# Two-block transformer chain on one core: where the modulation rows are reduced, who squares, and how the output stage starts

## The chip, the cores and the metric

The kernel runs on one core of a Trainium2 chip. The time is device microseconds (us) of one execution, from the core's first to its last instruction and a little around it. Of each version several executions are timed; one more is profiled, and all rows below come from that one.

## The reference, cut to what matters

The input is one sequence of 512 positions and 1024 features, held feature-major. Two stacks of two layers follow each other; everything is float32.

```
for l in range(2):                                       # first stack ("block 1")
    mod = silu(c) @ ada_w[l] + ada_b[l]                  # 9 vectors of 1024
    h += 0.5*mod * swiglu(norm(h), ffn_w_in[l,0], ffn_w_out[l,0])     # d_ff 2816
    z = norm(h) @ mix_w_in[l]                            # q,k,v | gates | u,v | two merge gates
    y_a = attention(...);  y_b = u * (W_s layernorm(v) + b)
    merged = sigmoid(zga)*(y_a @ proj_a) + sigmoid(zgb)*(y_b @ proj_b)
    h += mod * (merged @ w_out)
    h += 0.5*mod * swiglu(norm(h), ffn_w_in[l,1], ffn_w_out[l,1])
h = norm(h)
for i in range(2):                                       # second stack
    mod = silu(c_2) @ w_ada[i] + b_ada[i]; the same with c_ctx_2      # 6 vectors each
    x += gate * norm(mixer(norm(x)))                     # i=0: pooling, i=1: attention
    x += gate * norm(square(relu(norm(x) @ w_mlp_in)) @ w_mlp_out)    # d_ff 4096
```

In the first layer of the second stack a context of 256 positions goes through the same pooling and the same MLP as the latents. `mod` is a matrix times one vector: 240 "rows", each a block of 128 output features by 1024 inputs.

## The kernel before, in words

**Products.** Each float32 product is made of three: high times high, high times low and low times high, where a high part is the value rounded to `fp32r` and a low part what is left. TensorE (PE) so runs three matmuls per 128-row block (lines L584 to L586, and L958 to L960 and L1007 to L1009 in the first pair of tiles of a network, L1218 to L1220 in the last tiles of one). The tiles `WH`, `WL` are the parts of a weight, `nH`, `nL` of a normed input, `hH`, `hL` of a hidden tile, `mH`, `mL` of the merged activations, `ybH`, `ybL` of the gated branch.

**Slots.** All large weights come as 308 slots in a fixed list, each 128 partitions by up to 2048 elements. A slot goes through three steps: SyncE (SP) issues its DMA into one of two `raw` buffers, ScalarE (ACT) makes `WH` (L476), VectorE (DVE) makes `WL` (L489), each in one of four buffers. The main loops of ACT, DVE and GpSimd (POOL) advance one slot at a time (`step_act`, `step_dve`, `step_pool`); in step k they split slot k+3, and that needs slot k-1 to be used up. SP in turn k issues slot k+5, and for that waits for both parts of slot k+3, which has the same `raw` buffer. In 18 of the slots of the context MLP POOL makes `WL` (L501).

**Rows.** The modulation rows are no work for TensorE. DVE multiplies a row tile `araw` with the broadcast condition `cB` and sums (L550). Rows 144 to 207 are needed for two conditions, and take two half operations into PSUM (L559), a small sum (L563) and L550. There are two `araw` buffers. `rows_after(k)` says how many rows are done by the end of step k: one more in each step, none in steps 196 to 231. In step k DVE first splits, then reduces the rows, then does the step's other work. SP issues in turn k, behind slot k+5, the rows up to one beyond those of step k, and each waits until DVE is done with the row two before it (`row(j)` in `sp_program`).

**A network of block 1** (`ffn_pe`, `ffn_act`, `ffn_dve`) has 33 slots. A round of six is: an a-step (two gate tiles, ACT: Silu, L1061), a b-step (two value tiles, DVE: product, L1112; ACT: high part, L1068; DVE: low part, L1118), again a and b, and two o-steps (four output tiles each, of the group of hidden tiles before; DVE adds them to `h`, L1185). All take their PSUM banks in turn from six. The middle networks are the second of layer 0 (slots 63 to 95) and the first of layer 1 (slots 96 to 128). Each ends with three slots in which all outputs are made in two halves of 256 positions (`network_end_pe`, "enter"), so that the next norm can begin.

**The MLPs of the second stack** use the same functions with `gated` false: ACT makes relu, DVE squares it (L1115), ACT makes the high part of the square, DVE the low part (L1118). The context's tiles are `scrc`, `hHc`, `hLc`, `mac`.

**The gated branch and the merge stage.** In `gmlp_dve` DVE evicts four tiles `sv` (L1821), multiplies (L1826) and makes low parts (L1828); PE makes `sv` in L1771 with only two free banks. The merge stage has sixteen slots; ACT makes a sigmoid in one tile `scr` (L1856), DVE multiplies (L1878, L1881), adds (L1884), ACT makes `mH` (L1861), DVE `mL` (L1886). `output_end_pe` then makes the output tiles one after another, each over all eight `mH`, `mL`.

Of the kernel before, what the change touches and what calls it, by code (L numbers as in the profile page):

```python
# [6 lines left out]
F32 = mybir.dt.float32  # L7
# [8 lines left out]
S = 512  # L16
# [78 lines left out]


SHARED = [0, 0]
CHANGE = 8 * 18 - 16


def ada_plan():
# [239 lines left out]
def build(nc, A, out):  # L341
# [3 lines left out]
    with ctx:  # L345
# [157 lines left out]

        def rows_after(k):

            idle = max(0, min(k, SHARED[1] - 1) - SHARED[0] + 1)
            late = min(2, max(0, k - CHANGE + 1))
            return min(8 * len(adas), 17 + k - idle - late)  # L510

        def row_tile(j):
            return M.rows[j] if j < NE else M.araw[j % NA]
# [537 lines left out]
        def ffn_act(act, g, p, nf, gated, hH, open_end=False):  # L1051
            N = p.N
            chunks = ffn_chunks(nf)
            order = [(ci, f) for ci, (f0, cn) in enumerate(chunks) for f in range(cn)]

            def first(ci, f):
                n = 4 * ci + f
                act.wait_ge(*mm.to(g, "a", ci, f))
                if n >= 2:
                    act.wait_ge(*v_pr.to(g, "b", *order[n - 2]))  # L1060
                act.q.activation(p.scr[n % 2][:, 0:N], bank(g, "a", ci, f)[:, 0:N],  # L1061
                                 ACT.Silu if gated else ACT.Relu).then_inc(*empties(a_fn, g, "a", ci, f))
# [35 lines left out]
        def ffn_dve(dve, g, p, nf, gated, hH, hL, sink, open_end=False):  # L1098
# [4 lines left out]
            def product(ci, f):  # L1103
# [10 lines left out]
                else:  # L1114
                    dve.q.tensor_tensor(p.scr[2 + u][:, 0:N], p.scr[u][:, 0:N], p.scr[u][:, 0:N],  # L1115
                                        ALU.mult).then_inc(*v_pr.up(g, "b", ci, f))
                dve.wait_ge(*a_hhi.to(g, ci, f))
                dve.q.tensor_tensor(hL[:, ci % 2, f, :], p.scr[2 + u][:, 0:N], hH[:, ci % 2, f, :].bitcast(F32),  # L1118
                                    ALU.subtract).then_inc(*v_hlo.up(g, ci, f))

            def second(ci):
# [107 lines left out]
        def output_end_pe(g):  # L1229
# [3 lines left out]

            def group(pe, x, o):
                k, c = k0 + o // 2, lat.half[x].cols
                b, free = take(g, "O", x, o)
                pe.wait_ge(*a_whi.to(k))
                pe.wait_ge(*wlo(k))
# [1 line left out]
                         lambda i: (a_hhi.to(g, "m", i), v_hlo.to(g, "m", i)), (g, "O", x, o), free)  # L1240
                if x and o % 2:
                    mm.again("slot", k)
            return group


# [11 lines left out]
        def enter_act(act, l, j):  # L1257
# [4 lines left out]
            rows_act(act, rows_after(k0) + 1)  # L1262
            both_halves_act(act, g, mod(1, l, 3 * j), lambda x, i: v_h.to(prev, "O", x, i),
                            output_ahead(k0) if j == 2 else network_ahead(k0))

        def enter_dve(dve, l, j):
# [528 lines left out]
        def gmlp_dve(dve, g, l):  # L1795
# [19 lines left out]
            step_dve(dve)  # L1815
            step_dve(dve)
            dve.wait_ge(*ld_bsb.to(l))
            for f in range(4):
                v = M.vf[:, f, :].rearrange("p (a b) -> p a b", a=4)
                dve.wait_ge(*mm.to(g, "sv", f))  # L1820
                dve.q.tensor_tensor(v, bank(g, "sv", f)[:, :].rearrange("p (a b) -> p a b", a=4),  # L1821
                                    M.bsb[:, f, :].unsqueeze(1).broadcast_to([128, 4, 128]), ALU.add
                                    ).then_inc(*empties(v_ev, g, "sv", f))
                dve.wait_ge(*v_ev.to(g, "sv", f))
                dve.wait_ge(*a_ev.to(g, "uv", f))
                dve.q.tensor_tensor(M.vf[:, f, :], M.vf[:, f, :], M.uu[:, f, :], ALU.mult).then_inc(*v_ev.up(g, "uv", f))  # L1826
                dve.wait_ge(*a_yhi.to(g, "yb", f))
                dve.q.tensor_tensor(M.ybL[:, f, :], M.vf[:, f, :], M.ybH[:, f, :].bitcast(F32), ALU.subtract  # L1828
                                    ).then_inc(*v_ylo.up(g, "yb", f))

        def gmlp_pool(pool, g, l):
            pool.wait_ge(*mm.to(g, "v", 7, 0))
# [9 lines left out]
                                 ALU.mult).then_inc(*p_wT.up(g))  # L1842

        def merged_act(act, g):
            sg = lat.scr[0]
            before = None
            for m in range(4):
                for which in range(2):
                    if m or which:
                        step_act(act)  # L1850
                        step_act(act)
                    for f in (2 * m, 2 * m + 1):
                        act.wait_ge(*mm.to(g, "z", which, f))
# [4 lines left out]
                        before = (g, "sum", f) if which else (g, "p", 0, f)  # L1858
                        if which:
                            act.wait_ge(*v_mg.to(g, "sum", f))  # L1860
                            act.q.activation(M.mH[:, f, :], lat.scr[1 + f % 2][:, :], ACT.Copy  # L1861
                                             ).then_inc(*a_hhi.up(g, "m", f))

        def merged_dve(dve, g):
            sg = lat.scr[0]
            for m in range(4):
                for which in range(2):
                    if m or which:
                        step_dve(dve)
                        step_dve(dve)  # L1870
                    for f in (2 * m, 2 * m + 1):
                        y = lat.scr[1 + f % 2]
# [759 lines left out]
        def sp_program(sp):  # L2632
# [33 lines left out]
            loaded = 16  # L2666
            for k in range(len(slots)):
                if k == CHANGE:
# [136 lines left out]
```

## Time and profile before

| | |
|---|---|
| median of 3 executions | 3921.39 us (3918.61 to 3925.29) |
| profiled execution, its own time | 3915.16 us |
| its span | 3913.4 us |
| mean granted TensorE clock | 0.962 |
| PE busy | 3668.9 us (94%) |
| DVE busy | 2231.8 us (57%) |
| ACT busy | 1311.4 us (34%) |
| POOL busy | 341.8 us (9%) |
| moved by DMA | 451.93 MB, 115 GB/s over the span |

The matmuls overlap in this view, so "PE busy" is the time in which at least one is in the array; what PE loses is seen where a matmul row names an idle time before it. The two clock levels are 2.4 GHz (1.0) and 1.2 GHz (0.5).

### The profile page before, as it was taken

The page shows a single profiled execution, that of the slowest core. Times are in us where ns is not written, and L with a number is a line of the kernel's source. Part 1 is how long each engine was busy: PE and PEld are TensorE (multiplying, and loading weights), DVE is VectorE, ACT ScalarE, POOL GpSimd, SP SyncE. Part 2 cuts the span into 40 slices and gives each one's busy share as a digit, 9 for nine tenths or more (in the row PEclk, how much of TensorE's full clock was granted, in tenths as well). Part 3 has the DMA queues.
Part 4 walks back from the last instruction along what each step waited for, and adds up shares of the span by engine and source line. Part 5 has one row for each costly group of instructions (what it writes and reads, how often), then busy time and mean ns, then how long its engine had stood idle before and what let it go on. Part 6 is the DMA issues. An engine that isn't in the chain of part 4 may idle for free.

```text
span 3913.4 us, 45537 instructions
## 1 busy us (share of the span) xinstructions
PE 3668.9 (94%) x18026; PEld 2962.2 (76%) x18026; DVE 2231.8 (57%) x3607; ACT 1311.4 (34%) x1906; POOL 341.8 (9%) x380
## 2 busy tenths in 40 slices
PE   6999899999999999999999999887799969999997
PEld 5888856788889888855788878777588846577886
DVE  5554644656446545554666767776755555634444
ACT  3222443233223222444224323344322234533221
POOL 0000122000001000112001010134100010200000
PEclk9999999999999999989999999998899968999998
DMA  5433301334432433310343434333233311012221
GB/s 225 167 145 145 120 33 59 127 137 164 146 145 102 183 139 144 126 69 25 124 162 124 149 143 161 124 119 140 87 145 145 135 49 54 1 44 85 89 97 42
DMA packets 84228, 451.93 MB, mean 115 GB/s; under 512 B 10193, under 2 KB 10641, under 8 KB 47153
## 3 DMA queue, kind: packets, MB, share of 16 engines
q1 hardware_dynamic: 81936, 439.35, 30.5%
q0 software_dynamic: 2080, 9.67, 0.7%
q8 instruction: 144, 2.36, 0.2%
q14 instruction: 68, 0.55, 0.0%
HBM read 446.88 MB, written 2.10 MB: 115 GB/s over the span
## 4 chain that ended last, share of the span: by engine, by line
PE 80%; DVE 9%; issue 4%; ACT 4%; DMA 1%; POOL 1%; SPq 0%; DVEq 0%; POOLq 0%; ACTq 0%
PE ps L584 21%; PE ps L586 21%; PE ps L585 21%; PE ps L1453 3%; PE ps L1489 2%; ACT WH L476 1%; DVE WL L489 1%; DVE scrc L1115 1%; PE ps L2418 1%; PE ps L1471 1%; DMA araw<-in_ast 1%; DVE scr L661 1%; PE ps L2392 1%; PE ps L958 1%; PE ps L604 1%
## 5 line engine op out<-in xcount | busy, mean ns | idle before, releaser
L584 PE MATMUL ps<-nH,WH 128*128 128x512 f32 x2416 | 956.9, 396 | 9.2 <-DVE nL L716 7.1
L489 DVE TENSOR_TENSOR WL<-raw,WH 128x2048 fp32r<-128x2048 f32 (+2 forms) x290 | 639.2, 2208 | 555.8 <-ACT WH L476 554.7
L586 PE MATMUL ps<-nH,WL 128*128 128x512 f32 x2416 | 953.1, 395 | 0.0
L585 PE MATMUL ps<-nL,WH 128*128 128x512 f32 x2416 | 951.0, 394 | 0.0
L476 ACT ACTIVATE WH<-raw 128x2048 fp32r<-128x2048 f32 (+2 forms) x308 | 560.0, 1823 | 583.8 <-PE ps L586 554.4
L584 PEld LDWEIGHTS ps<-nH,WH 128*128 128x128 f32 x2416 | 457.7, 189 | 118.7 <-issue 10.4
L585 PEld LDWEIGHTS ps<-nL,WH 128*128 128x128 f32 x2416 | 457.6, 189 | 103.5 <-issue 2.2
L586 PEld LDWEIGHTS ps<-nH,WL 128*128 128x128 f32 x2416 | 457.3, 189 | 99.4
L584 PE MATMUL ps<-hH,WH 128*128 128x512 f32 x1072 | 422.2, 394 | 2.2 <-DVE h L1185 2.2
L586 PE MATMUL ps<-hH,WL 128*128 128x512 f32 x1072 | 421.8, 393 | 0.0
L585 PE MATMUL ps<-hL,WH 128*128 128x512 f32 x1072 | 421.5, 393 | 0.0
L550 DVE SCALAR_TENSOR_TENSOR araw<-araw,cB 128x1024 f32<-128x1024 f32 x225 | 276.5, 1229 | 73.3 <-DMA araw<-in_ast 73.2
L1068 ACT ACTIVATE hH<-scr 128x512 fp32r<-128x512 f32 x152 | 96.1, 632 | 456.7 <-DVE scr L1112 382.9
L584 PEld LDWEIGHTS ps<-hH,WH 128*128 128x128 f32 x1072 | 201.4, 188 | 48.5 <-DVE h L1185 2.7
L585 PEld LDWEIGHTS ps<-hL,WH 128*128 128x128 f32 x1072 | 201.4, 188 | 46.2
L586 PEld LDWEIGHTS ps<-hH,WL 128*128 128x128 f32 x1072 | 201.4, 188 | 46.2
L1061 ACT ACTIVATE scr<-ps 128x512 f32<-128x512 f32 x152 | 89.5, 595 | 387.5 <-PE ps L586 379.2
L931 POOL TENSOR_SCALAR scr<-scr,der,mods 128x256 f32<-128x256 f32 x80 | 61.8, 773 | 1532.9 <-DVE scr L844 1532.0
L1118 DVE TENSOR_TENSOR hL<-scr,hH 128x512 fp32r<-128x512 f32 x152 | 105.3, 692 | 106.1 <-ACT hH L1068 106.1
L1185 DVE SCALAR_TENSOR_TENSOR h<-ps,der,h 128x512 f32<-128x512 f32 x144 | 102.6, 747 | 66.9 <-PE ps L586 65.4
L2108 DVE TENSOR_TENSOR ma<-ma,ps 128x512 f32<-128x512 f32 x112 | 74.7, 684 | 111.6 <-PE ps L586 111.2
L1664 DVE TENSOR_REDUCE st<-ps 128x1 f32<-128x128 f32 (+3 forms) x128 | 62.0, 486 | 111.1 <-PE ps L1455 111.0
(357 smaller groups left out, 5432.6 us busy)
## 6 DMA issues: line engine op xcount, KB each, us to landing
raw<-in_wst SPq DMA_DIRECT2D x282, 1024.0 KB, 4.8
araw<-in_ast SPq DMA_DIRECT2D x225, 512.0 KB, 5.7
raw<-in_wst SPq DMA_DIRECT2D x18, 512.0 KB, 3.6
row<-in_ast SPq DMA_DIRECT2D x15, 512.0 KB, 15.0
cw<-in_cw POOLq DMA_DIRECT2D x4, 1024.0 KB, 6.0
h<-in_xT SPq DMA_DIRECT2D x1, 2048.0 KB, 8.3
raw<-in_wst SPq DMA_DIRECT2D x8, 256.0 KB, 2.6
out<-h SPq DMA_DIRECT2D x8, 256.0 KB, 2.0
```

What stands on the lines that cost most here:

```text
L476: act.q.activation(M.WH[k % NW][:, 0:n], M.raw[k % NR][:, 0:n], ACT.Copy).then_inc(*a_whi.up(k))
L489: dve.q.tensor_tensor(M.WL[k % NW][:, 0:n], M.raw[k % NR][:, 0:n], M.WH[k % NW][:, 0:n].bitcast(F32), ALU.subtract).then_inc(*v_wlo.up(k))
L550: dve.q.scalar_tensor_tensor(out=w[:, :], in0=w[:, :], scalar=1.0, in1=M.cB[q][:, :], op0=ALU.mult, op1=ALU.mult, accum_out=total).then_in ...
L584: pe.q.matmul(to, hi[:, i, cc], xh, start=i == 0, stop=False)
L585: pe.q.matmul(to, hi[:, i, cc], xl, start=False, stop=False)
L586: t = pe.q.matmul(to, lo[:, i, cc], xh, start=False, stop=i == nk - 1)
L1061: act.q.activation(p.scr[n % 2][:, 0:N], bank(g, "a", ci, f)[:, 0:N], ACT.Silu if gated else ACT.Relu).then_inc(*empties(a_fn, g, "a", ci, f))
L1068: act.q.activation(hH[:, ci % 2, f, :], p.scr[2 + f % 2][:, 0:N], ACT.Copy).then_inc(*a_hhi.up(g, ci, f))
L1118: dve.q.tensor_tensor(hL[:, ci % 2, f, :], p.scr[2 + u][:, 0:N], hH[:, ci % 2, f, :].bitcast(F32), ALU.subtract).then_inc(*v_hlo.up(g, ci, f))
L1185: dve.q.scalar_tensor_tensor(out=M.h[:, o, :], in0=bank(g, "o", ci, o)[:, :], scalar=gate[:, o:o + 1], in1=M.h[:, o, :], op0=ALU.mult, op1 ...
L1453: pe.q.matmul(b[:, 0:nk], M.q[half, hh // 2, 128 * qt:128 * qt + 128], K[half, 0:nk], start=True, stop=False, skip_group_check=True)
L1489: t = pe.q.matmul(to[half, 128 * x:512], M.Vt[br - 1][:, x, 64 * grp:64 * grp + 64], M.PT[br - 1][:, x, 128 * x:512], start=br == 1 and x ...
```

## The change

There are three parts, and two that go with them.

1. `rows_after(k)` reads a table made by `row_steps`. By it two rows are reduced in each step of the middle networks, and in every third step of layer 0's first network. None is reduced in the three last slots of a network (but for the fourth network, layer 1's second), in the first six slots of `mix_w_in`, in `proj_a`, `proj_b`, `w_out`, and in the first slots of the fourth network. The whole stays the same 240 rows. The extra row at the entry of a stage goes.
2. In the MLPs of the second stack ACT makes the high part as the square of relu itself, and no longer waits for DVE's product. In all networks DVE does two products and then two low parts.
3. The first four output tiles behind the merge stage are made together: all four over `mH`, `mL` 0 to 5, then all four over 6 and 7. It takes its four banks at once.
4. The merge stage uses two sigmoid tiles in turn, and in the gated branch the low part of a tile comes after the next tile's product.

```diff
-CHANGE = 8 * 18 - 16
+def row_steps(slots, total):
+    done, out, waited = 16, [], 0
+    for k, (a, idx, r0, nk, c0, n) in enumerate(slots):
+        more = 2 if a[:3] == "ffn" and (idx in ((0, 1), (1, 0)) or k % 3 == 0 and idx == (0, 0)) else 1
+        if a == "ffn_w_out" and r0 >= 16 * 128 and idx != (1, 1):
+            more = 0
+        if a == "ffn_w_in" and (c0 == NF * 128 or idx == (1, 1) and c0 % (NF * 128) < 512):
+            more = 0
+        if a == "mix_w_in" and c0 <= 1280 or a in ("proj_a", "proj_b", "w_out"):
+            more = 0
+        if SHARED[0] <= k < SHARED[1]:
+            more = 0
...
         def rows_after(k):
-            idle = max(0, min(k, SHARED[1] - 1) - SHARED[0] + 1)
-            late = min(2, max(0, k - CHANGE + 1))
-            return min(8 * len(adas), 17 + k - idle - late)
+            return row_plan[k]
...
             def high(ci, f):
-                act.wait_ge(*v_pr.to(g, "b", ci, f))
+                act.wait_ge(*(v_pr.to(g, "b", ci, f) if gated else a_fn.to(g, "a", ci, f)))
...
-                act.q.activation(hH[:, ci % 2, f, :], p.scr[2 + f % 2][:, 0:N], ACT.Copy).then_inc(*a_hhi.up(g, ci, f))
+                act.q.activation(hH[:, ci % 2, f, :], p.scr[(2 if gated else 0) + f % 2][:, 0:N],
+                                 ACT.Copy if gated else ACT.Square).then_inc(*a_hhi.up(g, ci, f))
...
                     product(ci, f)
                     product(ci, f + 1)
+                    low(ci, f)
+                    low(ci, f + 1)
...
+            def four(pe):
+                c, to = lat.half[0].cols, []
+                for o in range(4):
+                    b, free = take(g, "O", 0, o)
+                    pe.wait_ge(*free)
+                    to.append(b[:, 0:S // 2])
+                for part in (range(6), range(6, 8)):
+                    for o in range(4):
...
+                        for i in part:
+                            pe.wait_ge(*a_hhi.to(g, "m", i))
+                            pe.wait_ge(*v_hlo.to(g, "m", i))
...
-            rows_dve(dve, rows_after(k0) + 1)
+            rows_dve(dve, rows_after(k0))
...
         def merged_act(act, g):
-            sg = lat.scr[0]
-            before = None
+            before = [(), ()]
...
+                        sg = lat.scr[3 * (f % 2)]
                         act.wait_ge(*mm.to(g, "z", which, f))
-                        if before is not None:
-                            act.wait_ge(*v_mg.to(*before))
+                        if before[f % 2]:
+                            act.wait_ge(*v_mg.to(*before[f % 2]))
```

The order of the instructions shows part 1 in the middle networks. First SP, in the second network of layer 0, before the change; `raw` is a slot, `araw` a row, the number behind each name its buffer.

```order
L2647 DMA araw1_16<-in_ast 128x1024
L2639 DMA raw0_5<-in_wst 128x2048
L2647 DMA araw0_15<-in_ast 128x1024
L2639 DMA raw1_6<-in_wst 128x2048
L2647 DMA araw1_16<-in_ast 128x1024
```

The same place after the change:

```order
L2696 DMA raw1_6<-in_wst 128x2048
L2704 DMA araw0_15<-in_ast 128x1024
L2704 DMA araw1_16<-in_ast 128x1024
L2696 DMA raw0_5<-in_wst 128x2048
L2704 DMA araw0_15<-in_ast 128x1024
L2704 DMA araw1_16<-in_ast 128x1024
```

Two rows now stand behind each slot. DVE in the same network before the change, one a-step and one b-step:

```order
L489 TENSOR_TENSOR WL_13<-raw_5,WH_9 128x2048
L550 SCALAR_TENSOR_TENSOR araw_16,mods<-araw_16,cB_17 128x1024
L489 TENSOR_TENSOR WL_14<-raw_6,WH_10 128x2048
L550 SCALAR_TENSOR_TENSOR araw_15,mods<-araw_15,cB_17 128x1024
L1112 TENSOR_TENSOR scr_27<-scr_25,ps 128x512
L1118 TENSOR_TENSOR hL<-scr_27,hH 128x512
L1112 TENSOR_TENSOR scr_28<-scr_26,ps 128x512
L1118 TENSOR_TENSOR hL<-scr_28,hH 128x512
```

And after it:

```order
L512 TENSOR_TENSOR WL_13<-raw_5,WH_9 128x2048
L572 SCALAR_TENSOR_TENSOR araw_16,mods<-araw_16,cB_17 128x1024
L572 SCALAR_TENSOR_TENSOR araw_15,mods<-araw_15,cB_17 128x1024
L512 TENSOR_TENSOR WL_14<-raw_6,WH_10 128x2048
L572 SCALAR_TENSOR_TENSOR araw_16,mods<-araw_16,cB_17 128x1024
L572 SCALAR_TENSOR_TENSOR araw_15,mods<-araw_15,cB_17 128x1024
L1135 TENSOR_TENSOR scr_27<-scr_25,ps 128x512
L1135 TENSOR_TENSOR scr_28<-scr_26,ps 128x512
L1144 TENSOR_TENSOR hL<-scr_27,hH 128x512
L1144 TENSOR_TENSOR hL<-scr_28,hH 128x512
```

Each step has a second row, in the other `araw` buffer, ahead of the step's own work, and the low parts stand behind both products. ACT in the context's MLP, before the change, where `scrc_99` and `_100` hold relu and `scrc_101` and `_102` the squares:

```order
L476 ACTIVATE WH_7<-raw_5 128x2048
L1061 ACTIVATE scrc_99<-ps 128x256
L1068 ACTIVATE hHc<-scrc_101 128x256
L1061 ACTIVATE scrc_100<-ps 128x256
L1068 ACTIVATE hHc<-scrc_102 128x256
```

And after it:

```order
L499 ACTIVATE WH_7<-raw_5 128x2048
L1083 ACTIVATE scrc_99<-ps 128x256
L1090 ACTIVATE hHc<-scrc_99 128x256
L1083 ACTIVATE scrc_100<-ps 128x256
L1090 ACTIVATE hHc<-scrc_100 128x256
```

The order is the same; the high part now reads relu's own tile.

## Rows read from the trace of the kernel before

**Rows 1.** Windows: stretch, length, busy us per engine (count): PE, PEld, DVE, ACT, POOL; clock, DMA share, GB/s.
```profile
905.00:1205.00 300.00, 300.00 (x1318) 246.35 (x1317) 150.66 (x167) 78.27 (x71) 0.00 (x0) 1.00 0.42 156
...
2500.00:2755.00 255.00, 203.03 (x1470) 195.74 (x1470) 187.16 (x245) 106.01 (x145) 96.20 (x37) 0.89 0.37 130
...
839.00:843.00 4.00, 4.00 (x25) 4.00 (x25) 3.14 (x2) 2.24 (x3) 0.00 (x0) 0.65 0.00 0
```

**Rows 2.** Waits over the span: who for whom, us, times, longest.
```profile
DVE araw L550 <- DMA araw<-in_ast: 73.2, 24, 6.3
```

**Rows 3.** Timeline, DVE, entry behind layer 1's first network: start, us, engine, line, operation [idle before].
```profile
1586.72 1.22 DVE L550 SCALAR_TENSOR_TENSOR araw<-araw,cB 128x1024 f32<-128x1024 f32 x1
...
1593.03 1.23 DVE L550 SCALAR_TENSOR_TENSOR araw<-araw,cB 128x1024 f32<-128x1024 f32 x1 [5.08 <-DMA araw<-in_ast]
```

**Rows 4.** Timeline, SP, the same place.
```profile
1586.88 0.33 SPq L2639 DMA_DIRECT2D raw<-in_wst  x1
1587.25 0.43 SPq L2647 DMA_DIRECT2D araw<-in_ast  x1
```

**Rows 5.** DMA issues of 940 to 1180 (KB each, us to landing), and all row tiles.
```profile
raw<-in_wst SPq DMA_DIRECT2D x23, 1024.0 KB, 4.7
araw<-in_ast SPq DMA_DIRECT2D x23, 512.0 KB, 5.7
DMA to landing us min/median/max: 3.4/5.7/15.1
```

**Rows 6.** Timeline, DVE, one b-step.
```profile
1007.79 2.29 DVE L489 TENSOR_TENSOR WL<-raw,WH 128x2048 fp32r<-128x2048 f32 x1 [8.01 <-ACT WH L476]
...
1011.26 0.69 DVE L1112 TENSOR_TENSOR scr<-scr,ps 128x512 f32<-128x512 f32 x1
...
1016.34 0.69 DVE L1112 TENSOR_TENSOR scr<-scr,ps 128x512 f32<-128x512 f32 x1 [3.01 <-PE ps L586]
...
1019.60 2.29 DVE L489 TENSOR_TENSOR WL<-raw,WH 128x2048 fp32r<-128x2048 f32 x1 [1.18 <-ACT WH L476]
```

**Rows 7.** Groups by line, DVE, 940 to 1180: count, busy us, mean ns, idle before.
```profile
L1185 DVE SCALAR_TENSOR_TENSOR h<-ps,der,h 128x512 f32<-128x512 f32 x27 | 19.5, 748 | 15.9 <-PE ps L586 15.6
```

**Rows 8.** Timeline, DVE, a row for two conditions, and what follows it.
```profile
1639.12 0.69 DVE L559 SCALAR_TENSOR_TENSOR ps<-araw,cB 128x512 f32<-128x512 f32 x1
...
1641.89 1.16 DVE L1595 COPY R<-cm 64x496 f32<-64x496 f32 x2
```

**Rows 9.** Timeline, DVE, the first steps of layer 0's second network.
```profile
904.17 1.22 DVE L550 SCALAR_TENSOR_TENSOR araw<-araw,cB 128x1024 f32<-128x1024 f32 x1
```

**Rows 10.** Timeline, PE, the same place: the first row behind the wide pair.
```profile
906.17 0.40 PE L584 MATMUL ps<-nH,WH 128*128 128x512 f32 x1
```

**Rows 11.** Timeline, DVE, the first compression of layer 0.
```profile
445.13 2.33 DVE L1595 COPY R<-cm 64x496 f32<-64x496 f32 x4
```

**Rows 12.** Timeline, PE, the same place.
```profile
448.83 1.51 PE L1378 MATMUL ps<-R,cw 128*128 128x62 f32 x6 [9.29 <-DVE R L1599]
```

**Rows 13.** Timeline, PE, the gated branch of layer 0.
```profile
711.32 1.58 PE L1771 MATMUL ps<-wT,vn 128*64 128x128 f32 x16 [2.43 <-DVE vf L1821]
...
716.84 0.47 PE L584 MATMUL ps<-nH,WH 128*128 128x512 f32 x1 [1.23 <-DVE vf L1821]
```

**Rows 14.** Timeline, PE, the first output tile behind layer 0's merge stage.
```profile
836.11 0.36 PE L584 MATMUL ps<-mH,WH 128*128 128x256 f32 x1 [0.86 <-DVE mL L1886]
...
838.82 0.36 PE L584 MATMUL ps<-mH,WH 128*128 128x256 f32 x1 [2.12 <-DVE mL L1886]
```

**Rows 15.** Timeline, PE, the context's first sum.
```profile
2150.60 0.99 PE L619 MATMUL ps<-ones,scrc 128*128 128x1 f32 x4 [8.85 <-DVE scrc L661]
```

**Rows 16.** Timeline, DVE, the context's MLP.
```profile
2602.36 4.75 DVE L1115 TENSOR_TENSOR scrc<-scrc 128x256 f32<-128x256 f32 x1 [1.38 <-ACT scrc L1061]
...
2638.40 0.42 DVE L1115 TENSOR_TENSOR scrc<-scrc 128x256 f32<-128x256 f32 x1
```

**Rows 17.** Timeline, POOL, the same place.
```profile
2602.23 4.60 POOL L501 TENSOR_TENSOR WL<-raw,WH 128x2048 fp32r<-128x2048 f32 x1 [6.47 <-PE ps L586]
```

More of the change, by code:

```diff
@@ L97 @@
 SHARED = [0, 0]
-CHANGE = 8 * 18 - 16
+def row_steps(slots, total):
[10 more added lines that the diff above has]
+            more = 0
+        if done == 8 * 18 and waited < 2:
+            more, waited = 0, waited + 1
+        elif done < 8 * 18:
+            more = min(more, 8 * 18 - done)
+        done = min(total, done + more)
+        out.append(done)
+    return out
 def ada_plan():
@@ L502, in split_pool @@
                                      ALU.subtract).then_inc(*p_wlo.up(k))
+        row_plan = row_steps(slots, 8 * len(adas))
         def rows_after(k):
-            idle = max(0, min(k, SHARED[1] - 1) - SHARED[0] + 1)
-            late = min(2, max(0, k - CHANGE + 1))
-            return min(8 * len(adas), 17 + k - idle - late)
+            return row_plan[k]
         def row_tile(j):
@@ L1116, in product, with low @@
                                         ALU.mult).then_inc(*v_pr.up(g, "b", ci, f))
+            def low(ci, f):
                 dve.wait_ge(*a_hhi.to(g, ci, f))
-                dve.q.tensor_tensor(hL[:, ci % 2, f, :], p.scr[2 + u][:, 0:N], hH[:, ci % 2, f, :].bitcast(F32),
+                dve.wait_ge(*v_pr.to(g, "b", ci, f))
+                dve.q.tensor_tensor(hL[:, ci % 2, f, :], p.scr[2 + f % 2][:, 0:N], hH[:, ci % 2, f, :].bitcast(F32),
                                     ALU.subtract).then_inc(*v_hlo.up(g, ci, f))
@@ L1235, in group @@
                 k, c = k0 + o // 2, lat.half[x].cols
+                if x == 0 and o < 4:
+                    if o == 0:
+                        four(pe)
+                    return
                 b, free = take(g, "O", x, o)
@@ L1242, in group @@
                     mm.again("slot", k)
+            def four(pe):
[6 more added lines that the diff above has]
+                    for o in range(4):
+                        k = k0 + o // 2
+                        pe.wait_ge(*a_whi.to(k))
+                        pe.wait_ge(*wlo(k))
+                        hi, lo, cc = view(M.WH, k), view(M.WL, k), slice(o % 2 * 128, o % 2 * 128 + 128)
+                        for i in part:
+                            pe.wait_ge(*a_hhi.to(g, "m", i))
+                            pe.wait_ge(*v_hlo.to(g, "m", i))
+                            pe.q.matmul(to[o], hi[:, i, cc], M.mH[:, i, c], start=i == 0, stop=False,
+                                        skip_group_check=True)
+                            pe.q.matmul(to[o], hi[:, i, cc], M.mL[:, i, c], start=False, stop=False, skip_group_check=True)
+                            t = pe.q.matmul(to[o], lo[:, i, cc], M.mH[:, i, c], start=False, stop=i == 7,
+                                            skip_group_check=True)
+                        if i == 7:
+                            t.then_inc(*mm.up(g, "O", 0, o))
             return group
@@ L1261, in enter_act @@
             split_act(act, k0 + NW)
-            rows_act(act, rows_after(k0) + 1)
+            rows_act(act, rows_after(k0))
             both_halves_act(act, g, mod(1, l, 3 * j), lambda x, i: v_h.to(prev, "O", x, i),
@@ L1817, in gmlp_dve @@
             dve.wait_ge(*ld_bsb.to(l))
[L1818 to L1829, printed above, removed]
+            for f in range(5):
+                if f < 4:
+                    v = M.vf[:, f, :].rearrange("p (a b) -> p a b", a=4)
+                    dve.wait_ge(*mm.to(g, "sv", f))
+                    dve.q.tensor_tensor(v, bank(g, "sv", f)[:, :].rearrange("p (a b) -> p a b", a=4),
+                                        M.bsb[:, f, :].unsqueeze(1).broadcast_to([128, 4, 128]), ALU.add
+                                        ).then_inc(*empties(v_ev, g, "sv", f))
+                    dve.wait_ge(*v_ev.to(g, "sv", f))
+                    dve.wait_ge(*a_ev.to(g, "uv", f))
+                    dve.q.tensor_tensor(M.vf[:, f, :], M.vf[:, f, :], M.uu[:, f, :], ALU.mult).then_inc(*v_ev.up(g, "uv", f))
+                if f:
+                    dve.wait_ge(*a_yhi.to(g, "yb", f - 1))
+                    dve.q.tensor_tensor(M.ybL[:, f - 1, :], M.vf[:, f - 1, :], M.ybH[:, f - 1, :].bitcast(F32), ALU.subtract
+                                        ).then_inc(*v_ylo.up(g, "yb", f - 1))
         def gmlp_pool(pool, g, l):
@@ L1852, in merged_act @@
                     for f in (2 * m, 2 * m + 1):
+                        sg = lat.scr[3 * (f % 2)]
                         act.wait_ge(*mm.to(g, "z", which, f))
-                        if before is not None:
-                            act.wait_ge(*v_mg.to(*before))
+                        if before[f % 2]:
+                            act.wait_ge(*v_mg.to(*before[f % 2]))
                         act.q.activation(sg[:, :], bank(g, "z", which, f)[:, :], ACT.Sigmoid
                                          ).then_inc(*empties(a_fn, g, "z", which, f))
-                        before = (g, "sum", f) if which else (g, "p", 0, f)
+                        before[f % 2] = (g, "sum", f) if which else (g, "p", 0, f)
                         if which:
@@ L1864, in merged_dve @@
         def merged_dve(dve, g):
-            sg = lat.scr[0]
             for m in range(4):
@@ L1871, in merged_dve @@
                     for f in (2 * m, 2 * m + 1):
-                        y = lat.scr[1 + f % 2]
+                        y, sg = lat.scr[1 + f % 2], lat.scr[3 * (f % 2)]
                         dve.wait_ge(*a_fn.to(g, "z", which, f))
@@ L2665, in sp_program @@
                 raw(k)
-            loaded = 16
+            loaded, changed = 16, False
             for k in range(len(slots)):
-                if k == CHANGE:
+                if loaded == 8 * 18 + 1 and k and row_plan[k - 1] == 8 * 18 and not changed:
+                    changed = True
                     sp.wait_ge(*v_row.to(8 * 18 - 1))
```

## The prediction

> **What bounds the kernel now.** I read the clock and busy shares first, then windows of the stages, then the waits and the timelines behind them. The reader is to see that the kernel has two kinds of stages. In the middle networks PE has no idle time: 300 of 300 us busy, 1318 matmuls, 0.228 us each, DVE busy half the time [rows 1]. A slot of 48 matmuls is 10.98 us there, a round of six slots 65.9 us. So a step that DVE finishes sooner gains nothing, and DVE has 5 us a step to spare, if nothing makes it wait. Elsewhere PE waits: 52 of 255 us in the context's MLP [rows 1], and singly at the compression, in the gated branch and behind the merge stage [rows 12 to 14]. The question is whether DVE can take two rows a step in its spare time, and what their absence gives the other places.
>
> **Two rows a step.** DVE's time for the extra row, 1.26 us (1011.26 less 1007.79 less the 2.21 of the split [rows 6]), would fit. The wait for its data doesn't. With two `araw` buffers the step's second row can be issued only when the row two before is done, and SP has it behind the slot of the same turn, whose issue waits for `WL` of this very step. The trace has this case at stage entries, where two rows stand in one step: SP issues the slot 0.16 us after the first row has begun and the row 0.37 later [rows 4], it lands after 5.7 us, the median [rows 5], and the second row starts 6.31 us after the first, 5.08 of them idle [rows 3]. Between the bounds of 4.0 (the fastest landing, 3.4, with the 0.5 of issue before it) and 16 (the slowest, 15.1) I take 6.31, since it is this very sequence and agrees with the median; 24 such waits average 3.05 us [rows 2], but that counts single rows too.
>
> DVE's chain from split to split is then, in an a-step, 2.21 + 6.31 + 1.27 = 9.79 us; in a b-step 0.65 (first product) and 3.26 more, from the second product over the high part and ACT's next `WH` to the next split (1016.34 to 1019.60 [rows 6]): 13.7; in an o-step four sums of 0.7 (748 ns with its overlap [rows 7]): 12.6. A round is 2 x (9.79 + 13.7 + 12.6) = 72.2 against PE's 65.9. DVE falls back 6.3 us a round and becomes the bound. With rows for two conditions (144 to 207) the second takes 2.77 instead of 1.27 (1639.12 to 1641.89 [rows 8]); the first's longer time lies beside the landing. That is 1.5 more a step, 81.2 a round, 15.3 too long.
>
> Layer 0's second network: 28 double steps, slots 65 to 92 (10 a, 10 b, 8 o), 335.7 us. They begin late: the last split before ends at 904.17 [rows 9], two rows take until 911.8, then come the wide pair's products, so that the next split starts near 915.7, 10 after PE has left the wide pair at 906.17 [rows 10]. The first two splits come together (2.2 more), and a row then stands behind two slots, for which I estimate 1.6 more, little over the 1.3 by which 1 MB takes longer than the fastest row [rows 5]: 3.8. The last low part is made before a further split, 1.2 less. PE needs 28 x 10.98 = 307.4, and can do 1.4 us of the last slots first. Loss: 335.7 + 10 + 3.8 - 1.2 - 307.4 - 1.4 = 39.5.
>
> Layer 1's first network: eight double steps reach slot 104 some 16 us late, of which 3.9 is hidden: a sum into `h` ends that long before PE takes its bank again (the third output tile takes that of the first, 24 matmuls or 5.5 us later, less 1.6 of sums). 12 are paid. Slots 106 to 108 have one row or none and reset it. Slots 109 to 125 are 17 double steps with heavy rows (5 a, 6 b, 6 o): 49 + 82 + 76 + 17 x 1.5 = 232.3 against 186.7: 45. Together 57. PE's clock falls behind a long wait: right behind the waits in front of the first output tile it is 0.65 over 4 us [rows 1, 14], a loss of 1.4. I add 3 for the two network ends and take off 2 for waits that are there today. Sum of part 1's cost: 39.5 + 57 + 3 - 2 = 97, called 96 for the rounding of the small terms.
>
> The third-step extras in the first network cost nothing: a single late step per six is 1 to 2 us behind in a slot's 11, and the next ones catch up.
>
> **What the missing rows give.** At layer 0's compression DVE copies at 445.13 [rows 11], behind a burst of rows; without them it could at 439.2. PE starts at 448.83 [rows 12] and would at 442.7: 6.1, in layer 1 about 1. In the gated branch row and row wait go from between the tiles, and product stands ahead of low part: of waits like 2.43 and 1.23 [rows 13] nearly all goes, and the next product starts at 712.2 instead of 716.84: 4.7 a layer, 9.5. At the context's first sum PE waits 8.85 [rows 15]; without the row before the last squares 4.5 go. Other places with heavy rows: 2. Sum 23; the bounds are 10 (only the compression and half the branch) and 32 (every one of these waits gone).
>
> **Four output tiles together.** The waits of 0.86 and 2.12 [rows 14], 0.3 in others, and 1.7 of clock go, since PE has 72 matmuls of parts 0 to 5 before it needs 6. But it takes four banks at once; the fourth is that of a sigmoid which ACT makes in sequence near the end: a new wait of 1.6. Behind it stands all of PE, and nothing else is late. 3.6 in layer 0, 6.8 in layer 1, 10.4. Bounds: 4 (waiting 4.8 per layer) and 14.
>
> **High part by ACT.** ACT goes from relu's tile straight to the square, and needs no table for it (the norms' squares stand between relus today without one), so it costs nothing there; ACT is busy 106 of 255 us [rows 1]. What goes is the way over DVE, some 0.5 us per tile, more where DVE's product takes 4.75 instead of 0.42 us [rows 16] beside POOL's `WL` [rows 17]. PE waits for `hLc` all the same, which needs that product and the low part. Of 52 us I give it 10; bounds 0 and 25.
>
> That DVE product is what the Trainium skill ("GPSIMD Engine Reference", section "Specifications") would have: GpSimd shares its way to SBUF with VectorE, against instructions with two SBUF inputs. The trace agrees, 4.75 beside POOL against 0.42. By it only the high part gets out of the way, product and low part don't, which speaks against a gain much over 10.
>
> **Sum.** 3915.2 (the profiled execution's own time) + 96 - 23 - 10.4 - 10 = 3968. The median of the runs is 6 above the profiled one, which is not more than their spread; I take 3970.
>
> **Rivals.**
> A, the rows are hidden after all, faster. The chain fits into PE's round when the second row starts less than 5.28 us after the first (72.2 - 6 x 1.03 = 66). With the fastest landing, 3.4, it is 4.0, and a round takes 58 (68 heavy): loss 0 to 5, time 3921 - 43 + 3 = 3881. For it: the landing needed is only 1.03 shorter than the median, and the extra rows have shorter ones at times [rows 5]. Against it: in rows 3 a slot of 1 MB stands ahead of the row, as it would in every step, and that slot alone takes 4.7 [rows 5].
> B, only the heavy stretch pays: the first network's 38 are hidden by slots and banks prepared ahead. 3970 - 38 = 3932, still slower. For it: DVE idles 8.01 before a split [rows 6], so much slack there is at the start; against it: 39 is more than slack of that size.
> C, three transfers in a turn slow each other: landing 7.2 instead of 5.7, 0.5 MB more ahead of the row at the 1.3 us between the fastest row and a slot [rows 5], and a little. 1.5 x 50 steps = 75: 4045. For it: the slowest landing of 15.1; against it: the third is behind the second in one queue, and the queue is busy 42% of the time [rows 1].
> D, the gains don't come (the banks of the four tiles and POOL take them back), 20 instead of 43: 3993.
>
> The Trainium skill ("DMA: Bandwidth & Descriptors", section "Bandwidth") has 6.15 us for 1 MB, where the trace shows 4.7 [rows 5]. By it the row would come 1.4 later in 50 steps, an estimate of 70 us more, about 4040; the case is C's and has its chance. The measurement decides, so that the page is no part of the sum.
>
> **Numbers.** Forecast 0.58, A 0.15, B 0.11, C 0.08, D 0.08. Less than 0.2%, 8 us, can't be told from no change. Faster: A and little else, 0.16; within: the lower edge of B and the upper of A, 0.07; slower: 0.77. The forecast's own range is 3945 to 3995 (landing 0.3 us shorter or longer is 15). For 8 in 10 it reaches over B down to 3912 and up to 4012; A and C's upper part are left out.
>
> **What would show it.** DVE idle about 5 us for the row before the second of each pair, in some 55 steps; DVE's splits 36 us apart per three steps instead of 33; PE waiting at the third output tile of a round (a bank emptied by late sums) and for the last low parts at the network's ends, and a lower clock behind it; windows of the two networks some 39 and 57 us longer. On the other side: the compression's wait 9.3 down to about 3; no waits at the branch; a wait of 1.6 before the four tiles; the context's high part no more behind the product. The forecast is wrong if the wait before the second row is under 4 us, or if PE's matmuls in the networks stay at 0.229 us throughout.

## The result, and the profile after

| | before | after |
|---|---|---|
| median | 3920.0 us (3918.2 to 3925.29, 4 runs) | 3956.27 us (3953.55 to 3962.54, 4 runs) |
| ratio | 1 | 1.0093 (1.0075 to 1.011) |
| span of the profiled execution | 3913.4 us | 3952.6 us |
| clock | 0.962 | 0.959 |
| DVE waits for a row's DMA (L550/L572) | 73.2 us, 24 times [rows 2] | 257.9 us, 51 times |

The change makes the kernel 36 us slower. The forecast was 3970, inside 3912 to 4012. The two waits of DVE for rows after the change are these (who for whom, us in total, times, longest):

```profile
DVE araw L572 <- DMA araw<-in_ast: 257.9, 51, 7.2
DVE ps L581 <- DMA araw<-in_ast: 63.2, 18, 4.1
```

The first is what [rows 2] were before, three and a half times as much; the second is the same for rows with two conditions. The windows of the two middle networks and of the context's MLP (columns as in [rows 1]; the stretches are where these parts lie in the changed kernel):

```profile
890.00:1230.00 340.00, 316.08 (x1340) 257.26 (x1340) 180.30 (x222) 77.55 (x71) 0.00 (x0) 0.96 0.47 178
1284.00:1670.00 386.00, 340.86 (x1501) 280.04 (x1500) 243.17 (x411) 92.16 (x88) 5.63 (x8) 0.94 0.42 158
2556.00:2792.00 236.00, 202.22 (x1495) 195.47 (x1493) 183.32 (x239) 106.78 (x143) 95.53 (x37) 0.91 0.39 139
```

[rows 1] have layer 0's second network and the MLP; layer 1's first network was this, before:

```profile
1275.00:1585.00 310.00, 309.40 (x1366) 254.28 (x1365) 155.34 (x170) 81.22 (x73) 0.00 (x0) 1.00 0.41 152
```

PE, with 0 and 0.6 us of idle time before, is idle for 24 of 340 us in the first and 45 of 386 in the second; in the MLP it has 34 us of idle time in 236 where it had 52 in 255. Both profiles have the same number of matmuls, 18026, so that the same matmul can be looked up in each and its start subtracted. That gives where the 39 us between the profiles come from:

| stretch (time in the kernel before) | forecast | measured |
|---|---|---|
| layer 0, compression (430 to 450) | -6.1 | -6.6 |
| gated branch, layer 0 and 1 | -4.7, -4.7 | -4.7, -5.0 |
| merge stage's end and output tiles, layer 0 and 1 | -3.6, -6.8 | -1.8, -3.7 |
| layer 0's second network (906 to 1270) | +39.5 | +40.3 |
| layer 1's first network (1270 to 1640) | +57 | +58.8 |
| context's first sum (2135 to 2160) | -4.5 | -10.9 |
| context's MLP (2475 to 2780) | -10 | -18.0 |
| all else | -3 (and +1 in the networks, not split) | -9 |

The steps can be read one by one. DVE in a b-step and the a-step behind it, in layer 0's second network of the changed kernel (start, us, engine, line, operation, idle before):

```profile
1082.62 2.29 DVE L512 TENSOR_TENSOR WL<-raw,WH 128x2048 fp32r<-128x2048 f32 x1
1084.83 1.22 DVE L572 SCALAR_TENSOR_TENSOR araw<-araw,cB 128x1024 f32<-128x1024 f32 x1
...
1091.11 1.22 DVE L572 SCALAR_TENSOR_TENSOR araw<-araw,cB 128x1024 f32<-128x1024 f32 x1 [5.06 <-DMA araw<-in_ast]
1092.38 1.28 DVE L1135 TENSOR_TENSOR scr<-scr,ps 128x512 f32<-128x512 f32 x2
1093.77 1.29 DVE L1144 TENSOR_TENSOR hL<-scr,hH 128x512 fp32r<-128x512 f32 x2
1096.24 2.29 DVE L512 TENSOR_TENSOR WL<-raw,WH 128x2048 fp32r<-128x2048 f32 x1 [1.18 <-ACT WH L499]
1098.45 1.22 DVE L572 SCALAR_TENSOR_TENSOR araw<-araw,cB 128x1024 f32<-128x1024 f32 x1
...
1106.18 2.29 DVE L512 TENSOR_TENSOR WL<-raw,WH 128x2048 fp32r<-128x2048 f32 x1
```

SP in the same place:

```profile
1084.98 0.33 SPq L2696 DMA_DIRECT2D raw<-in_wst  x1
1085.36 1.05 SPq L2704 DMA_DIRECT2D araw<-in_ast  x2
```

The second row starts 6.28 us after the first (1084.83 to 1091.11), 5.06 of them idle, as at the stage entry of before (6.31 [rows 3]). SP issues the slot at 1084.98, 0.15 after the first row has begun (0.16 in [rows 4]), and two rows behind it, where [rows 4] had one. The first of the two is the row that DVE waits for. From split to split the b-step takes 13.62 us and the a-step 9.94; the forecast had 13.7 and 9.79. PE in the same kernel, at the third output tile of some rounds of either network, and at the last slots of both:

```profile
986.34 0.79 PE L606 MATMUL ps<-hH,WH 128*128 128x512 f32 x1 [5.97 <-DVE h L1213]
...
1058.46 0.50 PE L606 MATMUL ps<-hH,WH 128*128 128x512 f32 x1 [3.87 <-DVE h L1213]
...
1239.76 0.36 PE L1246 MATMUL ps<-hH,WH 128*128 128x256 f32 x1 [4.34 <-DVE hL L1144]
...
1544.98 0.80 PE L606 MATMUL ps<-hH,WH 128*128 128x512 f32 x1 [7.81 <-DVE h L1213]
...
1625.66 0.80 PE L606 MATMUL ps<-hH,WH 128*128 128x512 f32 x1 [7.71 <-DVE h L1213]
...
1666.21 0.55 PE L1246 MATMUL ps<-hH,WH 128*128 128x256 f32 x1 [9.81 <-DVE hL L1144]
```

The tile waits for DVE's sum, which empties its bank (5.97 and 7.81), the last slots for the last low part (4.34 and 9.81). A round of six slots took PE 72.1 us (986.34 to 1058.46), one with heavy rows 80.7 (1544.98 to 1625.66); DVE's chain was forecast at 72.2 and 81.2.

PE's waits explain only part of the loss. There are six of them in layer 0's second network, 28.3 us in all, and eight in layer 1's first, 45.1 us. The other 26 of the 99 us are matmuls at the lower of the two clock levels, right behind the waits. The window behind the wait of 5.97:

```profile
986.00:990.00 4.00, 3.66 (x9) 2.89 (x10) 4.00 (x5) 0.00 (x0) 0.00 (x0) 0.50 0.02 4
```

By 994 the clock is back at 1.00. On the side of the gains, PE at the compression, in the gated branch and in front of the four output tiles:

```profile
443.28 3.00 PE L1434 MATMUL ps<-R,cw 128*128 128x62 f32 x19 [3.33 <-DVE R L1655]
...
703.71 0.47 PE L606 MATMUL ps<-nH,WH 128*128 128x512 f32 x1 [0.44 <-DVE vf L1878]
...
821.66 0.36 PE L1292 MATMUL ps<-mH,WH 128*128 128x256 f32 x1 [1.64 <-DVE mL L1943]
```

The 9.29 of [rows 12] are 3.33, the 1.23 of [rows 13] 0.44, and the two waits of [rows 14] have become one of 1.64, about what the forecast put for the new wait of the four tiles. The 8.85 of [rows 15] are gone altogether.

### The profile page after: what moved, and what is told of

It is laid out like the page before. It is cut to its first block, busy times and chain, and to the rows that moved or that the text cites. A ratio compares the mean times of both kernels' runs of the same rounds, so it can differ in the third digit from the quotient of the medians.

```text
span 3952.6 us, 45843 instructions
## 1 busy us (share of the span) xinstructions
PE 3681.7 (93%) x18026; PEld 2972.0 (75%) x18026; DVE 2219.2 (56%) x3607; ACT 1311.8 (33%) x1906; POOL 342.0 (9%) x380
## 4 chain that ended last, share of the span: by engine, by line
PE 66%; DVE 12%; DMA 9%; issue 7%; ACT 5%; POOL 1%; SPq 0%; DVEq 0%; POOLq 0%; ACTq 0%
PE ps L606 16%; PE ps L608 16%; PE ps L607 16%; DMA araw<-in_ast 8%; DVE WL L512 4%; PE ps L1509 3%; ACT WH L499 2%; PE ps L1545 2%; PE ps L2475 1%; PE ps L1527 1%; PE ps L1246 1%; PE ps L1248 1%; PE ps L1247 1%; DVE ps L581 1%; DVE h L1213 1%
## 5 line engine op out<-in xcount | busy, mean ns | idle before, releaser
L606 PE MATMUL ps<-hH,WH 128*128 128x512 f32 x1072 | 433.1, 404 | 61.5 <-DVE h L1213 46.4
L572 DVE SCALAR_TENSOR_TENSOR araw<-araw,cB 128x1024 f32<-128x1024 f32 x225 | 276.7, 1230 | 258.0 <-DMA araw<-in_ast 257.9
L1138 DVE TENSOR_TENSOR scr<-scr 128x512 f32<-128x512 f32 x64 | 48.2, 756 | 158.4 <-ACT scr L1083 156.1
L581 DVE SCALAR_TENSOR_TENSOR ps<-araw,cB 128x512 f32<-128x512 f32 x128 | 88.6, 733 | 63.2 <-DMA araw<-in_ast 63.2
```

The costliest lines, as they stand in the source:

```text
L572: dve.q.scalar_tensor_tensor(out=w[:, :], in0=w[:, :], scalar=1.0, in1=M.cB[q][:, :], op0=ALU.mult, op1=ALU.mult, accum_out=total).then_in ...
L581: dve.q.scalar_tensor_tensor(out=banks[6 + x][:, :], in0=w[:, cut], scalar=1.0, in1=M.cB[q][:, cut], op0=ALU.mult, op1=ALU.mult, accum_out ...
L606: pe.q.matmul(to, hi[:, i, cc], xh, start=i == 0, stop=False)
```

## The experiments

All medians below are compared with the kernel before on the same chip (3918 to 3920 us); the ratio is to it. "Matmul by matmul" means the stretches of the table above, in the profiled executions.

### The parts without the row plan, and the row plan alone

The first kernel is the changed one with the rows as before:

```diff
-            return row_plan[k]
+            idle = max(0, min(k, SHARED[1] - 1) - SHARED[0] + 1)
+            late = min(2, max(0, k - CHANGE + 1))
+            return min(8 * len(adas), 17 + k - idle - late)
...
-            rows_dve(dve, rows_after(k0))
+            rows_dve(dve, rows_after(k0) + 1)
```

> The changed kernel with the rows of the kernel before (one per step, with the extra one at stage entries), so only squares, four tiles, two sigmoid tiles and the order of low parts are left of the change. Theory (the middle networks lose by the wait for each step's second row): both networks as before, no loss there (PE 0.229 us per matmul throughout); what is left is the context's MLP, up to 18 us, and the output stages, about 5: 3920 - 23 = 3897, range 3890 to 3908. Rival (product, product, low, low is what delays the networks): still 30 us or more lost in the two networks, about 3925 or more.

Measured: 3889.53 us (3888.2 to 3891.92), ratio 0.9931 (0.9915 to 0.9948). The rival is out: the networks take what they took before to within 1 us. The time is half a us under the range. Matmul by matmul, 18 to 19 us of the gain lie in the context's MLP (by where the stretch is begun), 2.5 at the context's first sum, 2.3 in the gated branches, 0.5 in layer 0's output stage and nothing in layer 1's.

The second is the kernel before with `row_steps` and without the rest:

```diff
-            return min(8 * len(adas), 17 + k - idle - late)
+            return row_plan[k]
```

> The kernel before with the new row plan alone. Theory: loses 99 us in the two middle networks (40 and 59) and gains some 30 at the compression, gated branch and the context's first sum: 3920 + 69 = 3989, range 3975 to 4000. Rival (the low parts' new order or the four tiles have a part in the loss): under 3975.

Measured: 4007.19 us (3996.29 to 4016.93), ratio 1.0229 (1.0204 to 1.0254). That is outside both expectations, on the far side. Matmul by matmul the networks lose 56.7 and 75.8 us, not 40 and 59. What is left between this and the changed kernel in the networks is the order of products and low parts; it has a part in the time, but the one opposite to the rival's. The experiment with that order alone is below. The gains of the rows alone are 6.6 at the compression, 10.9 at the context's first sum, 0.4 and 4.7 at the output stages, 2.6 and 2.8 in the gated branches: there rows and order are worth 4.7 and 5.0 together, and the order alone 0.9 and 1.5 (the first experiment).

### The rows ahead of the slot

Here SP issues the rows that step k reduces itself before slot k+5. The row waits only for the last row of step k-1, the slot for this step's split.

```diff
+                while loaded < rows_after(k):
+                    row(loaded)
+                    loaded += 1
                 if k + NR + NW - 1 < len(slots):
                     raw(k + NR + NW - 1)
```

> The changed kernel, where SP issues the rows that step k itself reduces ahead of slot k+5 instead of behind it; same rows, same buffers, same work on every other engine. Theory (the second row of a pair comes late because its issue stands behind a slot's, which waits for this step's own split): the second row is issued when the last row of the step before is done, about 3.5 us before it is wanted in an a-step and more in others; DVE's round falls from 72 to about 45 us, under PE's 65.9, and the networks' 99 us come back: 3956 - 97 = 3859, range 3850 to 3875. Rival 1 (DVE's own extra work and the queue's load are the cost): no more than 20 back, above 3935. Rival 2 (a row ahead of the slot delays the slots): the networks gain less, 3880 to 3920, with ACT waiting for raw.

Measured: 3855.0 us (3849.73 to 3855.97), ratio 0.9838 (0.9824 to 0.9853), as the theory had it, and far from both rivals. DVE in layer 0's second network of this kernel, one b-step:

```profile
1062.85 2.29 DVE L512 TENSOR_TENSOR WL<-raw,WH 128x2048 fp32r<-128x2048 f32 x1 [6.74 <-ACT WH L499]
1065.06 1.22 DVE L572 SCALAR_TENSOR_TENSOR araw<-araw,cB 128x1024 f32<-128x1024 f32 x1
1066.32 1.23 DVE L572 SCALAR_TENSOR_TENSOR araw<-araw,cB 128x1024 f32<-128x1024 f32 x1
1067.58 0.69 DVE L1135 TENSOR_TENSOR scr<-scr,ps 128x512 f32<-128x512 f32 x1
1071.40 0.69 DVE L1135 TENSOR_TENSOR scr<-scr,ps 128x512 f32<-128x512 f32 x1 [3.13 <-PE ps L608]
```

SP in the same place:

```profile
1065.21 0.33 SPq L2696 DMA_DIRECT2D raw<-in_wst  x1
1066.31 1.59 SPq L2704 DMA_DIRECT2D araw<-in_ast  x2
```

The second row now starts 1.26 us after the first, with no idle time, and DVE waits for PE again (3.13). The rows go out when a row is done (1066.31), and both are in the queue before the next slot. The waits for rows fall to this:

```profile
DVE araw L572 <- DMA araw<-in_ast: 21.2, 9, 4.2
```

Same rows, same buffers, same work: from 906 to 1640 of the kernel before, the networks now take 1.4 us less than there, 100 us less than in the changed kernel (40.3 + 58.8 + 1.4). So the whole loss came from one order of issues on SP's queue, and the lower clock behind PE's waits went with the waits.

### The order of low parts, alone

The changed kernel, with product, low, product, low as before:

```diff
                     product(ci, f)
-                    product(ci, f + 1)
                     low(ci, f)
+                    product(ci, f + 1)
                     low(ci, f + 1)
```

> The changed kernel (3956.3) with product, low, product, low as before, nothing else. Theory (a b-step of the middle networks now is 1.4 to 3 us shorter on DVE's chain, which bounds there): the networks lose 33 us more, as the rows alone showed: 3956 + 33 = 3989, range 3980 to 3995. Rival (what the rows alone lost more came from elsewhere): within 8 of 3956.

Measured: 3984.86 us (3970.59 to 3986.59), ratio 1.016 (1.014 to 1.018). The two networks lose 31.3 us more matmul by matmul, theory 33. A b-step of DVE (1083.80 to 1098.84) takes 15.04 us instead of 13.62, with 0.70 of idle time for ACT's high part before each low part. So where DVE is the bound, making both products first is worth 31 us; where PE is, as in the kernel before, it is worth nothing (the networks of the first experiment).

### Squares by ACT

The changed kernel with the high part of a square again as a copy of DVE's product:

```diff
-                act.wait_ge(*(v_pr.to(g, "b", ci, f) if gated else a_fn.to(g, "a", ci, f)))
+                act.wait_ge(*v_pr.to(g, "b", ci, f))
```

> The changed kernel with ACT's high part of the squares again a copy of DVE's product, all else kept. Theory A (the context's MLP gained 18 us because the high part no longer waits for DVE's product beside POOL's splits): 3956 + 15 = 3971, range 3966 to 3978, the loss all in that MLP. Theory B (it gained by the other order of products and low parts): within 5 of 3956.

Measured: 3973.47 us (3971.38 to 3975.66), ratio 1.0144 (1.0128 to 1.0159), as theory A had it. 16.5 us are lost in the context's MLP, under 0.1 us in the 600 us before it. The two profiles are 21.0 us apart; 2.8 of it lie behind the context's MLP, where the latents' squares are too, and no experiment says whether these have a part in it. ACT's high parts there, of this kernel (count, busy us, mean ns, idle before and who ended it):

```profile
L1090 ACT ACTIVATE hHc<-scrc 128x256 fp32r<-128x256 f32 x30 | 12.5, 417 | 63.6 <-DVE scrc L1137 63.6
```

And of the changed one:

```profile
L1090 ACT ACTIVATE hHc<-scrc 128x256 fp32r<-128x256 f32 x29 | 12.1, 418 | 0.9
L1138 DVE TENSOR_TENSOR scrc<-scrc 128x256 f32<-128x256 f32 x30 | 43.2, 1478 | 13.5 <-ACT scrc L1083 13.5
```

63.6 us of idle time in front of ACT's high parts are 0.9. DVE's product is as slow as before, 1478 ns in the mean where the short ones take 0.42 us [rows 16], and 13.5 us of waits for relu stay, but the product no longer holds up ACT, which has the next `WH` and relu behind it. PE's waits show what that gives: for ACT's relu they fall from 7.0 us with the copy to 0.5, and for the sums of the norm beside it (L683) from 22.9 to 13.5. Those for DVE's sums into `mac` rise from 12.7 to 15.4. That was the missed part: I priced the way of one tile through DVE, not ACT's queue behind the waiting high part.

### The four output tiles

On the kernel with rows ahead of the slot (3855.0), first without the four tiles:

```diff
-                if x == 0 and o < 4:
-                    if o == 0:
-                        four(pe)
-                    return
```

> The kernel with rows ahead of the slot (3855.0), without the four output tiles made together: each tile again over all eight parts, one after another. Theory (the rows that no longer stand in w_out shortened the last chain by themselves, and the four tiles exchange one wait for another): within 4 us of 3855. Rival (as the prediction had it, the four tiles give 10): 3865.

Measured: 3857.13 us (3840.12 to 3864.22), ratio 0.9837 (0.9805 to 0.9869). The two medians come from two chips and the runs of this kernel spread over 24 us, so they say little; matmul by matmul in the two output stages the four tiles are worth 1.5 to 2.5 us, not 10. PE waits once in each layer here, 1.95 us. In layer 0:

```profile
825.33 0.36 PE L606 MATMUL ps<-mH,WH 128*128 128x256 f32 x1 [1.95 <-DVE mL L1939]
```

Before, it waited 0.86 and 2.12 there [rows 14]. The first of these waits is gone with the row plan alone too, so it went with the rows, and I had given it to the four tiles. The two sigmoid tiles were not taken out by themselves; no run shows their share. Then with the bank of each tile taken when its first matmul comes:

```diff
-                    pe.wait_ge(*free)
-                    to.append(b[:, 0:S // 2])
+                    to.append((b[:, 0:S // 2], free))
                 for part in (range(6), range(6, 8)):
                     for o in range(4):
+                        if 0 in part:
+                            pe.wait_ge(*to[o][1])
```

> The kernel with rows ahead of the slot (3855.0), where the four tiles take each its bank when its first matmul comes instead of all four at the start. Theory (the 1.64 us in front of the four is the wait for the fourth bank, whose sigmoid comes last): that wait goes in both layers, 3855 - 3.3 = 3851.7, and up to 3 more where the clock no longer dips. Rival (the wait is for mL, as the row names its releaser): 3855, the wait stays.

Measured: 3847.74 us (3834.6 to 3848.95), ratio 0.9811 (0.9792 to 0.9829). The wait of 1.64 is gone in both layers, no wait over 0.4 us is left there, and these stretches are 1.9 and 0.8 us shorter matmul by matmul. The median is 1 us under the lowest that was expected (3848.7). The row had named `mL` as its releaser; it was the bank. The kernel with both sigmoids ahead of both `mH`:

```diff
-                        if which:
-                            act.wait_ge(*v_mg.to(g, "sum", f))
+                    for f in (2 * m, 2 * m + 1) if which else ():
+                        act.wait_ge(*v_mg.to(g, "sum", f))
```

> The one before with ACT making both sigmoids of a pair ahead of both mH. Theory: the sigmoid that frees the last bank no longer stands behind mH; nothing waits for it any more with banks in turn, so within 2 us of it. Rival (the last mH and mL come late): 1 us of wait ahead of parts 6 and 7 in each layer goes or comes.

Measured: 3850.96 us (3842.91 to 3855.38), ratio 0.9824 (0.9807 to 0.9841). The median is 3.2 us above that of the one before, less than the spread of either, and the two output stages agree within 0.1 us matmul by matmul: no difference that can be told. Last, the two best once more, on one chip:

> The kernel with rows ahead of the slot once more, beside the next one on one chip, to compare the two: 3855, range 3849 to 3859.

Measured: 3857.57 us (3851.24 to 3861.12), ratio 0.9844 (0.9828 to 0.9861).

> The same with banks in turn once more. Theory (the wait of 1.64 and the lower clock behind it in both layers): 4 to 7 us under the one beside it. Rival (the 7 us between their first medians was the spread of the clock in the attention stages): within 3.

Measured: 3846.95 us (3836.94 to 3850.39), ratio 0.9812 (0.9792 to 0.9832). This is 10.6 us below its neighbour. Banks in turn has the lowest median, 1.9% below the kernel before and 2.8% below the changed one. But the 10.6 us are more than the 4 to 7 expected, and the profiled executions of this pair do not show them: they are 0.9 us apart (spans of 3849.4 and 3848.6), with 0.8 and 0.9 us gained in the two output stages. What the waits and the two stretches show for the banks is 2 to 3 us. A candidate for the rest is the clock in the attention stages (last section), and whether the shorter wait has any part in that wasn't settled.

## Why the prediction was right, and where it was off

**The bound and the wait.** Right, and shown: the second row 6.28 us after the first (forecast 6.31), chains of 13.62 and 9.94 (13.7 and 9.79), networks +40.3 and +58.8 (39.5 and 57). The row of one stage entry carried 100 us of the sum, because it was the same sequence of issues. Taking the slot out from before the row takes the whole loss away: the second row then starts 1.26 us after the first, and the networks lose nothing. So A named the right condition, which this change did not meet; its limit of 5.28 us was not tested. Two things the forecast had not named. PE waits also for banks that DVE's product (L1135) empties, 4.12 us once in layer 0's network and 2.87, 5.75 and 2.31 in layer 1's. And the lower clock stands behind all but one of PE's fourteen waits in the networks, 26 of the 99 us, where the forecast had it at their ends only, within its 3. Both shift where the delay is paid and not its sum: the forecast took the loss from DVE's chain, and PE's rounds came out as long as that chain.

**B and C.** Layer 0's second network lost its 40, so B is out. The rows landed 6.1 us after issue in the stretch with double rows, in the median, against 5.7 before [rows 5]:

```profile
raw<-in_wst SPq DMA_DIRECT2D x17, 1024.0 KB, 4.8
araw<-in_ast SPq DMA_DIRECT2D x34, 512.0 KB, 6.1
```

That includes each pair's other row, issued 0.7 later, whose landing nobody waits for. The waited-for row landed after 5.7 to 5.8 (1085.36 to 1091.1), the slot in 4.8. C is out. The 6.15 us that the Trainium skill gives for 1 MB ("DMA: Bandwidth & Descriptors", section "Bandwidth") were measured with transfers issued by GpSimd. This kernel has four such transfers of 1 MB, over the whole span:

```profile
cw<-in_cw POOLq DMA_DIRECT2D x4, 1024.0 KB, 5.9
```

These land after 5.9 us, near the page's figure, but the slots are issued by SyncE and land after 4.8. So the estimate of 70 us more, worked out from that figure, was for the wrong issuer, and did not come.

**The gains** were 60, not 43. The step that failed is "Of 52 us I give it 10" for the context's MLP: it was 18.0, of which the squares by ACT were 16.5. The rule of the Trainium skill ("GPSIMD Engine Reference", section "Specifications"), that GpSimd and VectorE share their way to SBUF, agrees with the product's 1478 ns in the mean, but my use of it, as a reason against more gain, was wrong: the product stayed slow and cost less. The second is "4.5 go" at the context's first sum: 10.9 went, 10.9 by the rows alone and 2.5 without them. I had counted only the row before the last squares; under the new plan no rows stand in any of the six steps ahead, and PE no longer waits for the context's squares there. The third went the other way: 10.4 for the four tiles and the two sigmoids was 5.5, and the rows alone give 5.1 of it. In sum: 3 more lost in the networks, 5 less gained here, 8 and 6 more gained there, and 7 in stretches that I had given next to nothing, the attention stages among them.

## What to carry to other kernels

Before more work is put into a step, ask when its input can be issued, not only whether the engine has time: with two buffers and one queue, an item behind a transfer that waits for this same step arrives a full landing late. Here the cure was to issue it ahead of that transfer, which took no memory and no more work. If the same sequence stands even once in the old trace, the wait can be read there before the change is made. And a wait taken out of an engine's order frees all that stands behind it there; price that, not the one operation.

## What the runs showed of the hardware

The clock in the attention stages isn't the same from one execution to the next with the same instructions. Layer 0, 490 to 530, in the changed kernel (windows, columns as in [rows 1]):

```profile
490.00:530.00 40.00, 39.08 (x151) 20.34 (x150) 19.18 (x58) 19.48 (x50) 9.70 (x16) 0.83 0.08 27
```

And in two executions of the kernel with banks in turn, first the one with a span of 3832.8 us, then the one with 3848.6:

```profile
490.00:530.00 40.00, 39.08 (x178) 20.38 (x177) 22.38 (x69) 21.93 (x58) 11.81 (x20) 1.00 0.07 27
490.00:530.00 40.00, 39.09 (x154) 21.16 (x152) 18.00 (x53) 20.00 (x49) 8.94 (x15) 0.83 0.08 28
```

At 0.83 there are 151 matmuls in these 40 us, at 1.00 there are 178; over the whole attention stage it makes 6 us between the changed kernel and the first of the two, 7 in layer 1. Up to there the distance to the kernel before differs by under 1 us between them. The second execution of the same kernel has none of it: 13.8 of the 15.8 us between the two lie in the two attention stages. So executions of one kernel can differ by 14 us through places that no edit touches, and differences are to be read matmul by matmul within the edited stretch.
